# Low halves of 24 down-projection strips made by a negated copy on ACT and an adding SBUF-to-SBUF transfer

## The chip, the cores and the metric

The kernel runs on 1 core of one Trainium2 chip. The metric is the device time of one execution in microseconds (us). Three runs of the kernel before gave 1706.45, 1706.47 and 1707.92, so the median is 1706.47.

## What is computed

Two transformer blocks over 512 tokens of width 1024, all in float32. The first block has a gated MLP, a mixer (causal latent attention and a short convolution) and a second gated MLP; the second block has a mixer (Fourier, convolution, neighbourhood attention with a context) and a plain MLP. The change lies in that last MLP, whose core is

```python
hn = modulate_2(rms_norm_2(h_lat, norm2_g[i]), sh2, sc2)
h_lat = h_lat + g2 * (jnp.square(jax.nn.relu(hn @ mlp_w1[i])) @ mlp_w2[i])
```

with `mlp_w1` 1024 x 4096 and `mlp_w2` 4096 x 1024. A final RMS norm over the result is the output.

## The kernel before

Every large product is made in three passes on TensorE. A float32 value is split into a high half, rounded to the type float32r, and a low half, the value less its high half. TensorE then adds high weight x high activation, high weight x low activation and low weight x high activation (`products`, L779 to L781; for the seven products below L1316 to L1318).

**Strips.** Weights come in strips of 128 output columns: 128 partitions x 8 chunks x 128 columns, 512 KB. A strip has the running number u and the slot u % 4 in three rings of four: RAW (as loaded), W_HI and W_LO. Its way is: SP waits until the low half of strip u - 4 is ready and loads RAW (L571). ACT waits for the load and until TensorE is done with strip u - 4, and copies RAW to W_HI with rounding (`split_hi`, L1474; semaphore `hi_ready`). DVE subtracts, W_LO = RAW - W_HI (`split_lo`, L1958; for two strips in one instruction `split_pair`, L2492), and increments `lo_ready`. TensorE waits for `lo_ready` and for a free PSUM bank. The semaphores hi_ready and lo_ready count strips in order. ACT and DVE split three strips ahead (`LEAD`): `split_next(u0, it, j)` takes strip u0 + j + 3.

**The last MLP** is done in 4 parts of 1024 hidden columns. Each part has an up projection (8 strips of `mlp_w1`) and a down projection (8 strips of `mlp_w2`, starting at u + KC with u = U_MLP + 2 * KC * part). Part 0's up projection is made by plain strips: ACT makes the relu (L1798), DVE squares (L2559), ACT rounds (L1801), DVE subtracts (L2562). The up projections of parts 1 to 3 take strips in pairs, each pair by seven products of half size in place of eight (`seven_products`): DVE forms sums of weight quarters (`sum_weights`, L2481 to L2486, which also changes RAW in place at L2483), ACT rounds them, DVE subtracts (L2498). Three partial results are copied from PSUM to SG by ACT (`keep`, L1759); TensorE waits for these copies (`part_kept`) before it starts the third, fourth and fifth product, and DVE adds them back (L2504). Then ACT makes relu, square and rounding of the pair before (`finish_pair`, L1766 to L1788), and DVE the low halves (L2512, L2518).

The order on each engine is that of the program. In the last pair (i = 3) of parts 1 to 3 ACT does: keep 0, high half of down strip 0, keep 1, high half of down strip 1, keep 2, `finish_pair` of the pair before, `finish_pair` of the last pair, high half of down strip 2. During a down projection ACT splits strips 3 to 7 at j = 0 to 4, then the next up pair. DVE splits a strip, then updates X from the bank (L2545). In part 0's down projection DVE and ACT also prepare sums and differences of the normed activations for the seven products ("tau": DVE L2525 to L2531, ACT L1832, DVE L2538), for one chunk at each of j = 0 to 3; ACT's order there is high half of strip j + 3, then tau j. At j = 5 DVE makes the sums and the low halves of the next up pair, at j = 6 the low halves of the sums.

POOL (GpSimd) makes constants at the start and later only adds squares for the five norms (`sum_squares`, L756); the last of these runs in part 3's down projection. Nothing in the kernel before is loaded or stored by a DMA that POOL issues.

Of the kernel before, what the change touches and what calls it, by code (L numbers as in the profile page):

```python
# [5 lines left out]
F32 = mybir.dt.float32  # L6
F32R = mybir.dt.float32r
I32 = mybir.dt.int32
ALU = mybir.AluOpType
ACT = mybir.ActivationFunctionType  # L10
AX = mybir.AxisListType

P = 128
D = 1024
KC = D // P
# [5 lines left out]
H = 8  # L21
# [13 lines left out]
SPAN_IN = SPAN - SPAN % 16  # L35
# [8 lines left out]
RING = 4  # L44
# [19 lines left out]
U_MLP = U_OUT2 + KC  # L64
MLP_PARTS = 4
# [44 lines left out]
def block_pair_kernel(nc, a, out):  # L110

    with ExitStack() as ctx:
# [3 lines left out]
        def sb(name, shape, dt=F32, over=None):  # L116
            size = int(np.prod(shape[1:])) * 4
            offset = place[0] if over is None else over
            if over is None:
                place[0] += (size + 63) // 64 * 64  # L120
            t = nc.alloc_sbuf_tensor_at(name, shape, dt, offset=offset)
            where[name] = offset
            return t
# [12 lines left out]
        RAW = sb("RAW", [P, RING * STRIP])  # L136
        W_HI = sb("W_HI", [P, RING * STRIP], F32R)
        W_LO = sb("W_LO", [P, RING * STRIP], F32R)
# [71 lines left out]
        RPB = sb("RPB", [P, H * SPAN_IN + 16], over=scratch + 20 * 1024)  # L210
# [53 lines left out]
        def sem(name):  # L264
            return ctx.enter_context(nc.semaphore(name))

        raw_in = [sem(f"raw_in{i}") for i in range(RING)]
        hi_ready = sem("hi_ready")
        lo_ready = sem("lo_ready")
# [14 lines left out]
        const_ready = sem("const_ready")  # L284
# [58 lines left out]
        ctx_full = sem("ctx_full")  # L343
        chi_ready = sem("chi_ready")
        clo_ready = sem("clo_ready")
        flip_ready = sem("flip_ready")
        rpb_in = sem("rpb_in")
        table_in = sem("table_in")
        sig_ready = sem("sig_ready")
# [4 lines left out]
        ln_std = sem("ln_std")  # L354
        z_ready = sem("z_ready")
        act_ready = sem("act_ready")
        rpb_end = sem("rpb_end")
        table_split = sem("table_split")
        ut_mixed = sem("ut_mixed")
        swap_ready = sem("swap_ready")  # L360
# [44 lines left out]
        tau_hi = sem("tau_hi")  # L405
        tau_lo = sem("tau_lo")
        relu_done = sem("relu_done")
        EARLY, LATE = slice(0, HS), slice(HS, S)

        def chunk(t, k, n=S):  # L410
# [65 lines left out]
        def strip_of(t, slot):  # L476
            return t[:, slot * STRIP:(slot + 1) * STRIP]
# [246 lines left out]
        @block.gpsimd  # L724
        def _(pool):
            pool.memset(IDENT[:, :], 0.0).then_inc(pool_seq, 1)
            pool.memset(ONES[:, :], 1.0).then_inc(const_ready, 1)
            pool.memset(CONST[:, 0:1], EPS).then_inc(const_ready, 1)
            pool.memset(CONST[:, 1:2], LN_EPS).then_inc(const_ready, 1)
            pool.memset(CWIDE[:, :], 0.0).then_inc(const_ready, 1)  # L730
            pool.wait_ge(pool_seq, 1)
            pool.affine_select(out=IDENT[:, :], in_=IDENT[:, :], compare_op=ALU.not_equal, fill=1.0, base=0,
                               pattern=[[-1, P]], channel_multiplier=1).then_inc(ident_ready, 1)
            pool.wait_ge(ident_ready, 1)
            pool.tensor_tensor(SUM32[:, :], IDENT[:, 0:32], IDENT[:, 32:64], ALU.add).then_inc(pool_seq, 1)
            for i in (2, 3):
                pool.wait_ge(pool_seq, i)
                pool.tensor_tensor(SUM32[:, :], SUM32[:, :], IDENT[:, 32 * i:32 * i + 32], ALU.add).then_inc(pool_seq, 1)
            pool.wait_ge(pool_seq, 4)
            pool.sem_inc(const_ready, 1)  # L740
            pool.memset(FLIP[:, :], 0.0).then_inc(pool_seq, 1)
            pool.wait_ge(pool_seq, 5)
            pool.affine_select(out=FLIP[:, :], in_=FLIP[:, :], compare_op=ALU.not_equal, fill=-1.0, base=1 - P,
                               pattern=[[1, P]], channel_multiplier=1).then_inc(flip_ready, 1)
            sq, seq = Tally(sq_ready), Tally(pool_seq)
            seq.n = 5

            def sum_squares(clear):

                if clear:  # L750
                    pool.wait_ge(stat_ready, clear)
                pool.memset(SSUM[:, :], 0.0).then_inc(pool_seq, 1)
                pool.wait_ge(pool_seq, seq.add())
                for k in range(KC - 1):
                    pool.wait_ge(sq_ready, sq.add())
                    pool.tensor_tensor(SSUM[:, :], SSUM[:, :], SQ[:, k % 2 * S:(k % 2 + 1) * S], ALU.add).then_inc(pool_seq, 1)  # L756
                    pool.wait_ge(pool_seq, seq.add())
                    pool.sem_inc(sq_used, 1)
                sq.add()

            for norms in range(5):
                sum_squares(norms)
                if norms == 2:
                    pool.wait_ge(gem_done, T_2)
                    pool.memset(RPB[:, H * SPAN_IN:], 0.0).then_inc(rpb_end, 1)

        @block.tensor
        def _(pe):
# [220 lines left out]
            def ffn(u, after_up, after_down):  # L989
                for i, (_, chunks) in enumerate(FFN_PARTS):  # L990
                    if u == U_FFN0:
                        begin(u, H_HI, H_LO, normed())
                        strips(u + RING, 2 * chunks - RING, H_HI, H_LO)
                    elif i == 0:
                        new_strips(u, 2 * chunks, H_HI, H_LO, normed_halves(), first_halves)
                    else:
                        strips(u, 2 * chunks, H_HI, H_LO)
                    u += 2 * chunks
                    after_up[i]()
                    if u + KC == U_LATENT:  # L1000
                        strips(u, RING, A_HI, A_LO, chunks, each=widened(chunks))
                        for j in range(RING, KC - 1):
                            strip(u + j, (u + j) % RING, A_HI, A_LO, chunks)
                        last_halves(u + KC - 1, A_HI, A_LO, chunks)
                    else:
                        strips(u, KC, A_HI, A_LO, chunks, each=widened(chunks))
                    u += KC
                    after_down[i]()
# [147 lines left out]
            def mixer2():  # L1156
# [26 lines left out]
                def turn_biases(heads):  # L1183

                    for h in heads:
                        if h >= 5:
                            pe.wait_ge(bias_ready, h - 2)
                        pe.matmul(bank[BIAS_BANKS[h]][:, 0:SPAN], FLIP[:, :], RPB[:, h * SPAN_IN:h * SPAN_IN + SPAN],
                                  start=True, stop=True).then_inc(rpb_turned, 1)

                pe.wait_ge(table_in, 16 * (6 + ROWS))
                pe.wait_ge(bank_free, U_OUT2 + RING)
                pe.wait_ge(flip_ready, 1)
                pe.wait_ge(rpb_end, 1)
                turn_biases(range(2))
                turn_values(3)
                for t in range(2):
# [95 lines left out]
                for j in range(KC - 1):  # L1293
                    slot = (U_OUT2 + j) % RING
# [152 lines left out]
            for at, rows, n in ((16, ROWS1, V_ROWS), (128, ROWS2, M_CTX), (256, ROWS3, 2 * CK2)):  # L1447
# [13 lines left out]
            ffn(U_FFN1, [lambda: fold(64, M_2, T_ADA),  # L1461
                         nothing, lambda: fold(M_2, M_CTX, T_2)], [nothing, context, nothing])
            mixer2()
            mlp()
            tail()
# [3 lines left out]
        def _(act):  # L1469
            def split_hi(u, slot, turn):  # L1470

                act.wait_ge(raw_in[slot], turn * 16 + 16)
                act.wait_ge(strip_done, u + 1)
                act.activation(strip_of(W_HI, slot), strip_of(RAW, slot), ACT.Copy).then_inc(hi_ready, 1)  # L1474

            def split_next(u0, it, j):
                u = u0 + j + LEAD
                if not isinstance(it, int) or it * RING + u < STRIPS:
                    split_hi(it * RING + u, u % RING, it + u // RING)
# [414 lines left out]
            u = U_FFN0  # L1894
            for i, (_, chunks) in enumerate(FFN_PARTS):
                ffn_up(u, chunks)
                u += 2 * chunks
                down(u, 0 if i == 2 else None, True)
                u += KC
            mixer1()  # L1900
            norm_halves(48, U_OUT + KC)
            u = U_FFN1
            for i, (_, chunks) in enumerate(FFN_PARTS):
                ffn_up(u, chunks)
                u += 2 * chunks
                if i == 1:
                    act.wait_ge(ctx_in, 16)
                    for t in range(2):
# [4 lines left out]
                                   scale=1.0 / D).then_inc(ctx_std, 1)  # L1913
# [9 lines left out]
            def written(t):  # L1923
# [9 lines left out]
                           scale=1.0 / D).then_inc(tail_std, 1)  # L1933
# [7 lines left out]
                           scale=1.0 / D).then_inc(std_ready, 1)  # L1941
# [6 lines left out]
        def _(dve):  # L1948
# [5 lines left out]
                dve.wait_ge(dve_seq, seq.add())  # L1954

            def split_lo(u, slot):
                dve.wait_ge(hi_ready, u + 1)
                dve.tensor_tensor(strip_of(W_LO, slot), strip_of(RAW, slot), strip_of(W_HI, slot).bitcast(F32),  # L1958
                                  ALU.subtract).then_inc(lo_ready, 1)
# [528 lines left out]
            def split_pair(u):  # L2488

                at = slice(u % RING * STRIP, (u % RING + 2) * STRIP)  # L2490
                dve.wait_ge(hi_ready, u + 2)
                dve.tensor_tensor(W_LO[:, at], RAW[:, at], W_HI[:, at].bitcast(F32), ALU.subtract).then_inc(lo_ready, 2)  # L2492

            def split_sums(q):
# [296 lines left out]
```

## Time and profile before

| | |
|---|---|
| median of 3 runs | 1706.47 us |
| the profiled execution, its own time | 1709.55 us |
| its span | 1707.7 us |
| TensorE busy | 1682.7 us (99%) |
| DVE busy | 1148.6 us (67%) |
| ACT busy | 689.9 us (40%) |
| POOL busy | 67.3 us (4%) |

The profile comes from one execution. Busy time counts matmuls and other work, not waits or the issuing of DMAs. Durations of matmuls overlap, so their pace is read from their start times. In the rows, a line with an arrow says which line of which engine ended an engine's idle time. Part 0's down projection runs from 1400.0 to 1443.6 us, part 1's up projection to 1485.1 and its down projection to 1528.6; part 2's down projection starts at 1569.0, part 3's up projection at 1612.5.

### The profile page before, as it was taken

To read this page: it belongs to the slowest core of one execution; us is meant where nothing else is said; L and a number is where in the kernel's file an instruction comes from. 1 tells how busy PE (TensorE), PEld (TensorE's weight loads), DVE (VectorE), ACT (ScalarE), POOL (GpSimd) and SP (SyncE) were. 2 spreads that over 40 slices of the span, in tenths; PEclk is the share of its full clock that TensorE was granted. 3 is DMA by queue.
4 is the path that set the end of the run, shared out by engine and by line. 5 is a ranking of instruction groups with operands and counts; after the bars stand their busy time and mean duration, and the time that the engine had idled before them with its cause. 6 is when DMAs were issued, how large, how long until landed. Compare 5 with 4: busy or idle time off the path is not lost.

```text
span 1707.7 us, 24554 instructions
## 1 busy us (share of the span) xinstructions
PE 1682.7 (99%) x8956; PEld 1407.4 (82%) x8956; DVE 1148.6 (67%) x2096; ACT 689.9 (40%) x1048; POOL 67.3 (4%) x56
## 2 busy tenths in 40 slices
PE   7999999999999999999999999999999999999998
PEld 5788888888878868897888888888868988989897
DVE  3778578655655696469969973469675558756563
ACT  4421222234236573354222334342466443626262
POOL 0000000011000000200000000200000200000002
PEclk9999999999999999999999999999999999999999
DMA  9866566332523302537666632454200232434331
GB/s 331 254 207 197 178 202 211 109 102 57 141 74 98 99 1 75 172 106 219 190 204 188 175 113 80 116 167 112 87 1 17 83 112 74 116 87 124 85 108 50
DMA packets 355674, 218.59 MB, mean 128 GB/s; under 512 B 8544, under 2 KB 353668, under 8 KB 355588
## 3 DMA queue, kind: packets, MB, share of 16 engines
q1 hardware_dynamic: 355356, 217.37, 43.7%
q8 instruction: 52, 0.85, 0.2%
q14 instruction: 34, 0.28, 0.1%
q10 hardware_dynamic: 232, 0.09, 0.0%
HBM read 215.34 MB, written 2.11 MB: 127 GB/s over the span
## 4 chain that ended last, share of the span: by engine, by line
PE 91%; DVE 5%; ACT 1%; issue 1%; DMA 1%; SPq 0%; POOL 0%; DVEq 0%; ACTq 0%; POOLq 0%
PE bank L779 23%; PE bank L781 23%; PE bank L780 23%; PE bank L1316 2%; PE bank L1318 2%; PE bank L1317 2%; PE bank L1041 1%; PE bank L1025 1%; PE bank L957 1%; PE bank L961 1%; PE bank L958 1%; PE bank L1276 1%; DVE W_LO L1958 1%; DVE STAT L2172 1%; PE bank L1077 1%
## 5 line engine op out<-in xcount | busy, mean ns | idle before, releaser
L1474 ACT ACTIVATE W_HI<-RAW 128x1024 fp32r<-128x1024 f32 x278 | 292.3, 1055 | 458.7 <-PE bank L781 397.2
L779 PE MATMUL bank<-H_HI,W_HI 128*128 128x512 f32 x1090 | 425.6, 390 | 3.9 <-DVE W_LO L1958 3.8
L781 PE MATMUL bank<-H_HI,W_LO 128*128 128x512 f32 x1090 | 424.2, 389 | 0.0
L780 PE MATMUL bank<-H_LO,W_HI 128*128 128x512 f32 x1090 | 424.1, 389 | 0.0
L1958 DVE TENSOR_TENSOR W_LO<-RAW,W_HI 128x1024 fp32r<-128x1024 f32 x254 | 311.2, 1226 | 103.2 <-ACT W_HI L1474 100.0
L779 PE MATMUL bank<-A_HI,W_HI 128*128 128x512 f32 x714 | 279.4, 391 | 0.0
L780 PE MATMUL bank<-A_LO,W_HI 128*128 128x512 f32 x714 | 277.9, 389 | 0.0
L781 PE MATMUL bank<-A_HI,W_LO 128*128 128x512 f32 x714 | 277.9, 389 | 0.0
L779 PEld LDWEIGHTS bank<-H_HI,W_HI 128*128 128x128 f32 x1090 | 204.6, 188 | 49.3 <-issue 5.1
L781 PEld LDWEIGHTS bank<-H_HI,W_LO 128*128 128x128 f32 x1090 | 204.6, 188 | 42.6
L780 PEld LDWEIGHTS bank<-H_LO,W_HI 128*128 128x128 f32 x1090 | 204.6, 188 | 42.5 <-issue 0.2
L779 PEld LDWEIGHTS bank<-A_HI,W_HI 128*128 128x128 f32 x714 | 134.0, 188 | 28.4 <-issue 1.0
L781 PEld LDWEIGHTS bank<-A_HI,W_LO 128*128 128x128 f32 x714 | 134.0, 188 | 28.1
L780 PEld LDWEIGHTS bank<-A_LO,W_HI 128*128 128x128 f32 x714 | 134.1, 188 | 27.2
L1987 DVE SCALAR_TENSOR_TENSOR GACC<-GBUF,CSIL,GACC 128x256 f32<-128x256 f32 x360 | 147.5, 479 | 0.0
L756 POOL TENSOR_TENSOR SSUM<-SSUM,SQ 128x512 f32<-128x512 f32 x35 | 62.3, 1779 | 1590.7 <-ACT SQ L1485 1590.7
L2110 DVE TENSOR_TENSOR HF<-SG,bank 128x512 f32<-128x512 f32 x44 | 30.2, 686 | 127.9 <-PE bank L781 118.7
L1541 ACT ACTIVATE A_HI<-HF 128x512 f32 (+1 forms) x44 | 27.8, 633 | 204.2 <-DVE HF L2110 204.2
L2133 DVE SCALAR_TENSOR_TENSOR X<-bank,GHALF,X 128x512 f32<-128x512 f32 (+1 forms) x47 | 35.2, 748 | 39.2 <-PE bank L781 39.2
L2133 DVE SCALAR_TENSOR_TENSOR X<-bank,MOD,X 128x512 f32<-128x512 f32 x21 | 15.7, 749 | 58.3 <-PE bank L781 47.5
L2380 DVE SCALAR_TENSOR_TENSOR ACC<-CV,COL,ACC 128x512 f32<-128x512 f32 x60 | 45.0, 751 | 1.7
L2545 DVE SCALAR_TENSOR_TENSOR X<-bank,MOD,X 128x512 f32<-128x512 f32 x24 | 18.0, 748 | 40.9 <-PE bank L781 40.9
(432 smaller groups left out, 2311.6 us busy)
## 6 DMA issues: line engine op xcount, KB each, us to landing
RAW<-in_ffn_w SPq DMA_DIRECT2D x116, 512.0 KB, 4.9
GBUF<-in_w_ada SPq DMA_DIRECT2D x32, 1024.0 KB, 7.5
RAW<-in_mlp_w SPq DMA_DIRECT2D x64, 512.0 KB, 4.1
RAW<-in_w_in SPq DMA_DIRECT2D x57, 512.0 KB, 3.9
GBUF<-in_ada_w SPq DMA_DIRECT2D x24, 1024.0 KB, 7.2
RAW<-in_w_out SPq DMA_DIRECT2D x16, 512.0 KB, 3.9
RAW<-in_ffn_w SPq DMA_DIRECT2D x16, 384.0 KB, 3.4
PBUF<-in_w_ada SPq DMA_DIRECT2D x4, 1024.0 KB, 10.7
```

What stands on the lines that cost most here:

```text
L756: pool.tensor_tensor(SSUM[:, :], SSUM[:, :], SQ[:, k % 2 * S:(k % 2 + 1) * S], ALU.add).then_inc(pool_seq, 1)
L779: pe.matmul(dst, w_hi, x_hi, start=first and i == 0, stop=False)
L780: pe.matmul(dst, w_hi, x_lo, start=False, stop=False)
L781: mm = pe.matmul(dst, w_lo, x_hi, start=False, stop=last and i == len(blocks) - 1)
L1316: pe.matmul(dst, his[k], hi[k], start=first and k == 0, stop=False, skip_group_check=not first)
L1317: pe.matmul(dst, his[k], lo[k], start=False, stop=False, skip_group_check=not first)
L1318: mm = pe.matmul(dst, los[k], hi[k], start=False, stop=last and k == KC // 2 - 1, skip_group_check=not first)
L1474: act.activation(strip_of(W_HI, slot), strip_of(RAW, slot), ACT.Copy).then_inc(hi_ready, 1)
L1958: dve.tensor_tensor(strip_of(W_LO, slot), strip_of(RAW, slot), strip_of(W_HI, slot).bitcast(F32), ALU.subtract).then_inc(lo_ready, 1)
L1987: ins = dve.scalar_tensor_tensor(out=acc[k % 2], in0=g[:, k * GEM:(k + 1) * GEM], scalar=CSIL[:, vec + k:vec + k + 1], in1=acc[k % 2], op0 ...
L2133: dve.scalar_tensor_tensor(out=chunk(X, it * RING + j), in0=bank[(u0 + j) % RING][:, :], scalar=gate[:, bass.ds(it * RING + (gate0 + j), 1 ...
L2380: ins = dve.scalar_tensor_tensor(out=chunk(ACC, c), in0=v, scalar=tap, in1=chunk(ACC, c), op0=ALU.mult, op1=ALU.add)
```

## The change

For the 24 down strips of parts 0, 1 and 2 (the list `DOWNS`), DVE's subtraction is left out. After the high half, ACT waits for it to be complete and writes the negated high half into the strip's slot of W_LO. POOL waits for that, issues a DMA from SBUF to SBUF that adds RAW to W_LO in place, waits until it has landed, and increments `lo_ready`. Before the first strip of each part it also waits until all strips before it are counted. DVE waits for `lo_ready` before it splits the pair that follows a down projection, so that the count stays in order. Apart from this, two semaphores of constants (`flip_ready`, `rpb_end`) are merged into `const_ready`, which TensorE then awaits at 7. The transfers stand in POOL's program before the last sum of squares. The values computed are the same: -W_HI + RAW for RAW - W_HI.

```diff
--- before.py
+++ after.py
@@ -343,7 +343,6 @@
         ctx_full = sem("ctx_full")
         chi_ready = sem("chi_ready")
         clo_ready = sem("clo_ready")
-        flip_ready = sem("flip_ready")
         rpb_in = sem("rpb_in")
         table_in = sem("table_in")
         sig_ready = sem("sig_ready")
@@ -354,7 +353,6 @@
         ln_std = sem("ln_std")
         z_ready = sem("z_ready")
         act_ready = sem("act_ready")
-        rpb_end = sem("rpb_end")
         table_split = sem("table_split")
         ut_mixed = sem("ut_mixed")
         swap_ready = sem("swap_ready")
@@ -405,6 +403,9 @@
         tau_hi = sem("tau_hi")
         tau_lo = sem("tau_lo")
         relu_done = sem("relu_done")
+        neg_hi = sem("neg_hi")
+        lo_landed = sem("lo_landed")
+        DOWNS = [U_MLP + 2 * KC * part + KC + j for part in range(MLP_PARTS - 1) for j in range(KC)]
         EARLY, LATE = slice(0, HS), slice(HS, S)
 
         def chunk(t, k, n=S):
@@ -741,7 +742,7 @@
             pool.memset(FLIP[:, :], 0.0).then_inc(pool_seq, 1)
             pool.wait_ge(pool_seq, 5)
             pool.affine_select(out=FLIP[:, :], in_=FLIP[:, :], compare_op=ALU.not_equal, fill=-1.0, base=1 - P,
-                               pattern=[[1, P]], channel_multiplier=1).then_inc(flip_ready, 1)
+                               pattern=[[1, P]], channel_multiplier=1).then_inc(const_ready, 1)
             sq, seq = Tally(sq_ready), Tally(pool_seq)
             seq.n = 5
 
@@ -759,10 +760,19 @@
                 sq.add()
 
             for norms in range(5):
+                if norms == 4:
+                    for n, u in enumerate(DOWNS):
+                        slot = u % RING
+                        pool.wait_ge(neg_hi, n + 1)
+                        pool.dma_start(strip_of(W_LO, slot).bitcast(F32), strip_of(RAW, slot), accum_op=ALU.add).then_inc(lo_landed, 16)
+                        pool.wait_ge(lo_landed, 16 * (n + 1))
+                        if n % KC == 0:
+                            pool.wait_ge(lo_ready, u + RING)
+                        pool.sem_inc(lo_ready, 1)
                 sum_squares(norms)
                 if norms == 2:
                     pool.wait_ge(gem_done, T_2)
-                    pool.memset(RPB[:, H * SPAN_IN:], 0.0).then_inc(rpb_end, 1)
+                    pool.memset(RPB[:, H * SPAN_IN:], 0.0).then_inc(const_ready, 1)
 
         @block.tensor
         def _(pe):
@@ -1190,8 +1200,7 @@
 
                 pe.wait_ge(table_in, 16 * (6 + ROWS))
                 pe.wait_ge(bank_free, U_OUT2 + RING)
-                pe.wait_ge(flip_ready, 1)
-                pe.wait_ge(rpb_end, 1)
+                pe.wait_ge(const_ready, 7)
                 turn_biases(range(2))
                 turn_values(3)
                 for t in range(2):
@@ -1472,6 +1481,9 @@
                 act.wait_ge(raw_in[slot], turn * 16 + 16)
                 act.wait_ge(strip_done, u + 1)
                 act.activation(strip_of(W_HI, slot), strip_of(RAW, slot), ACT.Copy).then_inc(hi_ready, 1)
+                if isinstance(u, int) and u in DOWNS:
+                    act.wait_ge(hi_ready, u + 1)
+                    act.activation(strip_of(W_LO, slot), strip_of(W_HI, slot).bitcast(F32), ACT.Copy, scale=-1.0).then_inc(neg_hi, 1)
 
             def split_next(u0, it, j):
                 u = u0 + j + LEAD
@@ -1954,6 +1966,10 @@
                 dve.wait_ge(dve_seq, seq.add())
 
             def split_lo(u, slot):
+                if isinstance(u, int) and u in DOWNS:
+                    return
+                if isinstance(u, int) and u - 1 in DOWNS:
+                    dve.wait_ge(lo_ready, u + RING)
                 dve.wait_ge(hi_ready, u + 1)
                 dve.tensor_tensor(strip_of(W_LO, slot), strip_of(RAW, slot), strip_of(W_HI, slot).bitcast(F32),
                                   ALU.subtract).then_inc(lo_ready, 1)
@@ -2489,6 +2505,8 @@
 
                 at = slice(u % RING * STRIP, (u % RING + 2) * STRIP)
                 dve.wait_ge(hi_ready, u + 2)
+                if u - 1 in DOWNS:
+                    dve.wait_ge(lo_ready, u + RING)
                 dve.tensor_tensor(W_LO[:, at], RAW[:, at], W_HI[:, at].bitcast(F32), ALU.subtract).then_inc(lo_ready, 2)
 
             def split_sums(q):
```

## Rows read from the trace of the kernel before

**Rows 1.** The page: busy time of TensorE, and the two groups that split strips
```profile
PE 1682.7 (99%) x8956; PEld 1407.4 (82%) x8956; DVE 1148.6 (67%) x2096; ACT 689.9 (40%) x1048; POOL 67.3 (4%) x56
...
L1474 ACT ACTIVATE W_HI<-RAW 128x1024 fp32r<-128x1024 f32 x278 | 292.3, 1055 | 458.7 <-PE bank L781 397.2
...
L1958 DVE TENSOR_TENSOR W_LO<-RAW,W_HI 128x1024 fp32r<-128x1024 f32 x254 | 311.2, 1226 | 103.2 <-ACT W_HI L1474 100.0
```

**Rows 2.** Waits of TensorE, 1396 to 1660 us (us in total, times, longest)
```profile
PE bank L1316 <- ACT SG L1759: 0.6, 1, 0.6
```

**Rows 3.** Windows: us, busy PE, PEld, DVE, ACT, POOL (x count), clock, DMA share, GB/s
```profile
1400.00:1443.60 43.60, 43.60 (x194) 36.09 (x194) 32.58 (x45) 14.75 (x16) 0.00 (x0) 1.00 0.25 72
...
1485.10:1528.60 43.50, 43.50 (x194) 36.03 (x193) 20.48 (x22) 13.43 (x16) 0.00 (x0) 1.00 0.35 96
```

**Rows 4.** Timeline of TensorE (start us, us, engine line op, what, idle before)
```profile
1443.58 0.28 PE L1316 MATMUL bank<-H_HI,W_HI 128*128 128x256 f32 x1
...
1448.67 0.39 PE L1316 MATMUL bank<-H_HI,SUM_HI 128*128 128x256 f32 x1 [0.62 <-ACT SG L1759]
...
1479.33 0.28 PE L1316 MATMUL bank<-H_HI,SUM_HI 128*128 128x256 f32 x1
...
1480.77 0.28 PE L1316 MATMUL bank<-TAU_HI,SUM_HI 128*128 128x256 f32 x1
...
1485.09 0.40 PE L779 MATMUL bank<-A_HI,W_HI 128*128 128x512 f32 x1
```

**Rows 5.** Timeline of DVE, part 0's down projection and the pair after it
```profile
1411.15 1.23 DVE L1958 TENSOR_TENSOR W_LO<-RAW,W_HI 128x1024 fp32r<-128x1024 f32 x1 [1.86 <-ACT W_HI L1474]
1412.30 0.74 DVE L2545 SCALAR_TENSOR_TENSOR X<-bank,MOD,X 128x512 f32<-128x512 f32 x1
...
1416.34 0.42 DVE L2531 SCALAR_TENSOR_TENSOR TAU<-TAU,HSUM 128x256 f32<-128x256 f32 x1
1418.62 1.23 DVE L1958 TENSOR_TENSOR W_LO<-RAW,W_HI 128x1024 fp32r<-128x1024 f32 x1 [1.86 <-ACT W_HI L1474]
...
1445.19 0.75 DVE L2545 SCALAR_TENSOR_TENSOR X<-bank,MOD,X 128x512 f32<-128x512 f32 x1
...
1446.57 0.69 DVE L2483 TENSOR_TENSOR RAW<-RAW 128x512 f32<-128x512 f32 x1
```

**Rows 6.** Timeline of ACT: part 0's up projection, and first and last pair of part 1
```profile
1388.64 1.04 ACT L1474 ACTIVATE W_HI<-RAW 128x1024 fp32r<-128x1024 f32 x1
...
1448.26 0.36 ACT L1759 ACTIVATE SG<-bank 128x256 f32<-128x256 f32 x1
...
1476.65 0.38 ACT L1759 ACTIVATE SG<-bank 128x256 f32<-128x256 f32 x1 [3.19 <-PE bank L1318]
1476.93 1.05 ACT L1474 ACTIVATE W_HI<-RAW 128x1024 fp32r<-128x1024 f32 x1
1478.09 0.38 ACT L1759 ACTIVATE SG<-bank 128x256 f32<-128x256 f32 x1
...
1479.53 0.39 ACT L1759 ACTIVATE SG<-bank 128x256 f32<-128x256 f32 x1
...
1484.31 0.63 ACT L1776 ACTIVATE CROSS<-CROSS 128x512 f32<-128x512 f32 x1 [0.97 <-DVE CROSS L2504]
...
1487.65 1.99 ACT L1474 ACTIVATE W_HI<-RAW 128x1024 fp32r<-128x1024 f32 x2
```

**Rows 7.** The page: DMA issues, KB each and median us from issue to landing
```profile
RAW<-in_mlp_w SPq DMA_DIRECT2D x64, 512.0 KB, 4.1
...
GBUF<-in_ada_w SPq DMA_DIRECT2D x24, 1024.0 KB, 7.2
...
out<-YTOK SPq DMA_DIRECT2D x4, 512.0 KB, 3.0
CTOK<-in_ctx SPq DMA_DIRECT2D x1, 1024.0 KB, 6.2
```

**Rows 8.** POOL's additions (ns min/median/max)
```profile
L756 POOL TENSOR_TENSOR SSUM<-SSUM,SQ x35: 1287/1810/1987, 371.1 to 1694.4; 128x512 f32<-128x512 f32 x35
```

## The prediction, made before the changed kernel was run

> **What bounds the kernel now.** I read the page first. TensorE is busy for 1682.7 of 1707.7 us [rows 1], so only idle gaps of TensorE, 25 us in all, can be given back, and DVE (67%) and ACT (40%) count only where TensorE waits for them. The change touches the last MLP, so next comes the list of TensorE's waits there, from 1396 to 1660 us: one wait, 0.6 us, for the ACT copy of a partial product [rows 2]. The windows say the same: in the down projections of parts 0 and 1 TensorE is busy for all of the 43.6 and 43.5 us, with the granted clock at 1.00 (the level of 2.4 GHz) [rows 3]. There is almost nothing to win here, and the question is what the new path can cost.
>
> A strip of 24 matmuls takes 43.5 / 8 = 5.44 us; a pair of strips in an up projection takes seven products of 12 matmuls at 0.12 us, 10.08 us. In the TensorE timeline the fourth and fifth products of part 1's last pair begin at 1479.33 and 1480.77, 1.44 us apart, and the down projection at 1485.09 [rows 4].
>
> **DVE's side: what is removed.** 24 subtractions of 1.226 us [rows 1], 29.4 us of DVE. They matter only in part 0's down projection. There DVE's turn for one strip lasts 1418.62 - 1411.15 = 7.47 us, against TensorE's 5.44 [rows 5]: it waits for ACT's high half, subtracts, updates X, splits and makes a tau block, and ACT in turn rounds that tau block before the next high half. So DVE falls behind, and its last update starts at 1445.19 although the strip ended at 1443.6; the sum of raw weights that ACT waits for starts at 1446.57, ACT's next high half is late, its second kept product starts only at 1448.26 [rows 5, 6], and TensorE's fourth product starts at 1448.67 in place of 1443.58 + 4.32 = 1447.90 (0.77 us), with the first matmul at 0.22 in place of 0.12 us, and a smaller gap of the same sort at the fifth (0.35): 1.2 us in all. Without the subtraction DVE's turn is the rest of it, 1412.30 to 1416.34 + 0.42, 4.5 us [rows 5], and the wait for the tau high half (0.85 us on ACT, in part overlapped) still leaves it under 5.44. DVE then keeps up, the last update starts some 1.3 us earlier and the gap closes: -1.2 us. In parts 1 and 2 DVE is busy for 20 of 43.5 us [rows 3], and nothing is gained.
>
> **ACT's side: what is added.** 24 negated copies, of the shape of the high half, so 1.055 us each [rows 1], and each waits for the high half's completion first, some 0.1 us: 1.15 us a strip. In the down projection of part 0 ACT is busy for 14.75 of 43.6 us [rows 3], and that hides them. In part 0's up projection the first copy delays a relu by 1.1 us, which that relu's next wait for TensorE (1.66 us) absorbs. They are not hidden where strips 0 and 1 of the down projection are split between the kept products of the last pair, in parts 1 and 2 (part 3's down strips are not in the list). In order on ACT now [rows 6]: kept 0 at 1476.65, high half 1476.93 to 1477.98, kept 1 at 1478.09, high half, kept 2 at 1479.53. After the change: high half to 1477.98, negated copy 1478.08 to 1479.13, kept 1 at 1479.03 to 1479.41, so the fourth product starts at 1479.46, not 1479.33; with its slow first matmul 0.25 us. High half 1479.31 to 1480.36, negated copy 1480.46 to 1481.51, kept 2 ends at 1481.79, so the fifth product starts at 1481.84 where 1480.77 + 0.25 was due: 0.82, and 0.1 for its first matmul. Together 1.2 us a part, in two parts +2.4 us. The relu chain behind it starts at 1481.7 and not 1479.8, and its 3.5 us end at 1485.2, before the last pair's chain, which starts at 1484.31 [rows 6] plus the 1.2, so it costs nothing more. The bounds of this term: 0, if the kept copies have more room than the timeline shows, and 4.6, if each of the four copies costs its whole 1.15.
>
> **POOL and the DMA: what is added.** Each low half now needs a POOL-issued transfer that reads 512 KB of RAW and 512 KB of the negated half, and writes 512 KB. POOL handles them one at a time: wait for the copy, issue, wait for landing, increment. Call this L. No row shows such a transfer. From below: a 512 KB store out of SBUF lands 3.0 us after its issue. From above: a load of 1024 KB beside other traffic lands in 7.2 us. I take 5.2: the 3.0 plus what 512 KB more cost an undisturbed load, 6.2 for CTOK less about 4.0 for RAW (4.1 in the MLP) [rows 7]. How much time is there? Part 1, by the ACT times above, with the down projection starting at 1486.3 and strip j needed 5.44 j later:
> - Strip 0's copy is ready at 1479.1, so L may be 7.1.
> - Strip 2's high half is split with strip 3's from 1487.65 on [rows 6]; 1.2 us later, with the copy behind it, it is ready at 1491.0. Needed at 1497.1: L up to 6.1.
> - From there POOL's row of transfers counts. Strip 7, the sixth transfer from there, is needed at 1524.3: lateness 6L - 33.3, zero at L = 5.55. If strips 0 and 1 already push it, 8L - 45.2.
> - Part 0 begins earlier: strip 0's high half is split at 1388.64 [rows 6], the copy is ready at 1390.7, strip 7 is needed at 1438.1: 8L - 47.4, zero at 5.9.
>
> At 5.2 none of them is late, and the term is 0. Each RAW slot is refilled when its low half has landed, 4.1 us [rows 7]; the tightest refill (strip 6 in part 1) lands at 1491.0 + 5.2 + 4.1 = 1500.3, and ACT wants it at 1502.9. DVE has one new wait, before the pair behind each down projection, with the updates of strips 6 and 7 and the next sums queued behind it; in part 1 strip 7's copy is ready at about 1510.5 and lands long before 1521. SP's queue waits for the same landings. POOL has nothing else then; its next sum of squares is in part 3's down projection. The merged semaphores wait for events long past: 0.
>
> **The sum**: -1.2 + 2.4 + 0 = +1.2 us on this execution (1709.55 us, span 1707.7), 0.07%. The median of the runs is 1706.47, so 1707.6.
>
> **Rivals.**
> 1. POOL's row of transfers sets the pace (slower). It decides from L = 5.55 on in parts 1 and 2 and 5.9 in part 0. For it: my L is only 0.35 us under that, and every transfer runs beside loads that take 0.35 of the DMA engines [rows 3]. Against it: the transfer goes in long rows within SBUF, and the nearest 512 KB row takes 3.0. At L = 6.2: 2.2 + 2 x 4.4 = 11 us, 1718; at 7.2: 10.2 + 2 x 12.4 = 35, so 1743. The loss passes 0.2% from about L = 5.75. Chance 0.40.
> 2. POOL is held up by DVE. POOL's own additions of one shape take from 1287 to 1987 ns [rows 8], so something beside it costs up to 0.7 us. If that came onto the issue of each transfer, L = 5.9: 0 + 2 x 2.1 = 4.2, and 1.2, 1712. Chance 0.04. The Trainium skill (SBUF — State Buffer, "Who interferes with whom") speaks against the change here: POOL writes the descriptors of its DMAs, and shares a pair of SBUF ports with DVE under an exclusive lock. By the same section a DVE instruction with two SBUF inputs takes only the read side, and that page infers that descriptors need the write side; by that the subtractions around these transfers don't hold them.
> 3. DVE's relief is there and ACT's price is not: 1706.5 - 1.2 = 1705.3, same within the measurement. Chance 0.06, within "same". To get past 0.2% (3.4 us) faster, gaps would have to close that the waits don't list: 0.04.
>
> **How the numbers follow.** My forecast, no transfer late, has 0.46, with rival 3 beside it 0.52 for within 0.2%, about what a measurement of this kernel can tell from no change. Slower 0.44 (rivals 1 and 2), faster 0.04. The forecast's own range is 1705.3 to 1710. The whole range goes from 1705 to 1743, L = 7.2; beyond it I leave about 0.15 above and a few hundredths below.
>
> **What would show it.** POOL's queue: 24 transfers, each landing in about 5 us; over 5.5 is rival 1, and TensorE's waits then name the landing at the first matmul of down strips, from strip 2 on, growing to strip 7 in each part. The ACT steps: two waits of TensorE for SG, at the fourth and fifth product of the last pair, in parts 1 and 2, some 0.1 and 0.8 us; part 3 none. The DVE step: the wait at the first pair of part 1 is gone, and DVE's updates in part 0 come 5.4 us apart. I am wrong if L is over 5.8, if part 0's down projection has gaps of its own, or if loads of RAW become late behind the landings.

## The result, and the profile after

The changed kernel takes 1736.66 us (median of 4 runs, 1734.22 to 1737.08) against 1706.55 (median of 4), a ratio of 1.0172 with a 95% interval of 1.016 to 1.0185: 1.7% slower. The forecast was 1707.6 with a range of 1705 to 1743, so the time lies in the range, at its first rival and not at the forecast. Both profiled executions (spans 1707.7 and 1735.2 us) have a mean granted clock of 0.91 in their first 40 us, long before the changed code, while executions with 1.00 there are some 3 us shorter (spans of 1708.4 and 1705.6 us in runs 6 and 2 below), so the change is best read between the two profiled ones: 27.5 us, of the 30.1 us between the medians.

The page of the changed kernel, its busy time (to be read beside [rows 1]), its queues and its DMA issues:

```profile
span 1735.2 us, 24601 instructions
...
PE 1688.2 (97%) x8956; PEld 1405.7 (81%) x8956; DVE 1120.4 (65%) x2072; ACT 714.7 (41%) x1072; POOL 88.1 (5%) x80
...
q1 hardware_dynamic: 355356, 217.37, 43.2%
q0 software_dynamic: 3456, 12.58, 3.7%
...
RAW<-in_mlp_w SPq DMA_DIRECT2D x64, 512.0 KB, 4.3
...
W_LO<-RAW POOLq DMA_DIRECT2D x24, 512.0 KB, 6.5
```

DVE gave up 28 us of work and ACT took 25, as planned, and the kernel is slower all the same. The new row is the last: 24 transfers, each landing 6.5 us (median) after its issue.

The waits of TensorE from 1396 to 1690 us, where [rows 2] had one of 0.6 us:

```profile
PE bank L789 <- POOLq L771: 20.5, 17, 1.7
PE bank L1325 <- ACT SG L1771: 1.2, 2, 0.6
PE bank L789 <- DVE X L2563: 0.8, 1, 0.8
```

L771 is POOL's increment of `lo_ready` after a landing. The third row is one of the same stalls (strip 2 of part 1), put down to what came last by the profile. The stalls cost more than the rows say. The list has 18 gaps of 21.3 us in all, but the down projections of parts 0 to 2 grew by 7.9, 9.1 and 9.6 us, 26.6 in all. The rest, 0.3 us a gap, is the overlap of two matmuls that is lost and a slower first matmul behind the gap.

POOL's queue in part 0 and at the start of part 1 (start us, us of the issue, and the idle time before it with its releaser):

```profile
1390.97 1.01 POOL L767 DMA_DIRECT2D W_LO<-RAW  x1 [41.54 <-ACT W_LO L1486]
1396.23 0.86 POOL L767 DMA_DIRECT2D W_LO<-RAW  x1 [4.25 <-POOLq L771]
1404.28 0.86 POOL L767 DMA_DIRECT2D W_LO<-RAW  x1 [7.19 <-ACT W_LO L1486]
1411.33 0.86 POOL L767 DMA_DIRECT2D W_LO<-RAW  x1 [6.19 <-DMA W_LO<-RAW]
1418.38 0.86 POOL L767 DMA_DIRECT2D W_LO<-RAW  x1 [6.19 <-DMA W_LO<-RAW]
1425.22 0.86 POOL L767 DMA_DIRECT2D W_LO<-RAW  x1 [5.98 <-DMA W_LO<-RAW]
1432.12 0.86 POOL L767 DMA_DIRECT2D W_LO<-RAW  x1 [6.04 <-DMA W_LO<-RAW]
1439.16 0.86 POOL L767 DMA_DIRECT2D W_LO<-RAW  x1 [6.18 <-DMA W_LO<-RAW]
1486.03 0.86 POOL L767 DMA_DIRECT2D W_LO<-RAW  x1 [46.01 <-ACT W_LO L1486]
1491.12 0.86 POOL L767 DMA_DIRECT2D W_LO<-RAW  x1 [4.22 <-POOLq L771]
```

The first transfer of a part frees POOL after 5.26 and 5.09 us, the later ones come about 7.0 us apart. TensorE's timeline follows them, one gap for each strip of part 0 from strip 3 on (from strip 2 on in part 1, from strip 1 on in part 2):

```profile
1417.99 0.49 PE L789 MATMUL bank<-A_HI,W_HI 128*128 128x512 f32 x1 [1.32 <-POOLq L771]
1424.94 0.47 PE L789 MATMUL bank<-A_HI,W_HI 128*128 128x512 f32 x1 [1.22 <-POOLq L771]
1431.73 0.49 PE L789 MATMUL bank<-A_HI,W_HI 128*128 128x512 f32 x1 [1.07 <-POOLq L771]
1438.77 0.49 PE L789 MATMUL bank<-A_HI,W_HI 128*128 128x512 f32 x1 [1.31 <-POOLq L771]
1445.86 0.49 PE L789 MATMUL bank<-A_HI,W_HI 128*128 128x512 f32 x1 [1.38 <-POOLq L771]
```

Last, ACT between the kept products of part 1's last pair, which answers to [rows 6], and the starts of the fourth and fifth product:

```profile
1483.32 0.38 ACT L1771 ACTIVATE SG<-bank 128x256 f32<-128x256 f32 x1 [3.18 <-PE bank L1327]
1483.60 1.05 ACT L1483 ACTIVATE W_HI<-RAW 128x1024 fp32r<-128x1024 f32 x1
1484.68 1.06 ACT L1486 ACTIVATE W_LO<-W_HI 128x1024 fp32r<-128x1024 f32 x1
1485.65 0.37 ACT L1771 ACTIVATE SG<-bank 128x256 f32<-128x256 f32 x1
1485.91 1.05 ACT L1483 ACTIVATE W_HI<-RAW 128x1024 fp32r<-128x1024 f32 x1
1486.99 1.06 ACT L1486 ACTIVATE W_LO<-W_HI 128x1024 fp32r<-128x1024 f32 x1
1487.96 0.37 ACT L1771 ACTIVATE SG<-bank 128x256 f32<-128x256 f32 x1
```

```profile
1485.88 0.28 PE L1327 MATMUL bank<-TAU_HI,SUM_LO 128*128 128x256 f32 x1
1486.07 0.38 PE L1325 MATMUL bank<-H_HI,SUM_HI 128*128 128x256 f32 x1
1486.29 0.28 PE L1326 MATMUL bank<-H_LO,SUM_HI 128*128 128x256 f32 x1
...
1488.38 0.39 PE L1325 MATMUL bank<-TAU_HI,SUM_HI 128*128 128x256 f32 x1 [0.62 <-ACT SG L1771]
```

Kept 1 ends at 1486.02, and the fourth product starts 0.05 us later, at 1486.07, where 1486.00 was due; its first matmul takes 0.22 us to the next in place of 0.12. Together that is 0.17 us, too little for the list of waits. Kept 2 ends at 1488.33, and the fifth product starts 0.05 us later, 0.79 us after its time. By the starts of the strips the whole difference of the two profiled executions is accounted for, stage by stage:

| stage | before, us | after, us | difference |
|---|---|---|---|
| down projection, part 0 (its end) | 1443.58 | 1451.45 | +7.9 |
| up, part 1 | 41.51 | 41.34 | -0.2 |
| down, part 1 | 43.55 | 52.62 | +9.1 |
| up, part 2 | 40.31 | 41.35 | +1.0 |
| down, part 2 | 43.55 | 53.17 | +9.6 |
| up, part 3 | 40.31 | 40.31 | 0 |

The sum is 27.4 of 27.5 us. Part 2's up projection shows ACT's price alone, 1.0; in part 1 the same 1.0 and DVE's relief make -0.2, so the relief is 1.2. (Runs 4 and 8 below show the relief alone: part 1's up projection takes 40.31 us in place of 41.51.)

### The profile page after: what moved, and what is told of

It reads as the page before. It is cut to its first block and busy times, and to the rows that moved or that the text cites. A ratio compares the mean times of both kernels' runs of the same rounds, so it can differ in the third digit from the quotient of the medians.

```text
span 1735.2 us, 24601 instructions
## 1 busy us (share of the span) xinstructions
PE 1688.2 (97%) x8956; PEld 1405.7 (81%) x8956; DVE 1120.4 (65%) x2072; ACT 714.7 (41%) x1072; POOL 88.1 (5%) x80
## 3 DMA queue, kind: packets, MB, share of 16 engines
q1 hardware_dynamic: 355356, 217.37, 43.2%
## 5 line engine op out<-in xcount | busy, mean ns | idle before, releaser
L1974 DVE TENSOR_TENSOR W_LO<-RAW,W_HI 128x1024 fp32r<-128x1024 f32 x230 | 282.1, 1227 | 85.4 <-ACT W_HI L1483 82.1
L789 PE MATMUL bank<-A_HI,W_HI 128*128 128x512 f32 x714 | 281.4, 394 | 21.3 <-POOLq L771 20.5
```

The costliest lines, as they stand in the source:

```text
L789: pe.matmul(dst, w_hi, x_hi, start=first and i == 0, stop=False)
```

## The experiments

The question is where the 7.0 us come from, when the first transfer of a part took 5.1. Edits are against the changed kernel. The first four ran beside each other with the kernel before at 1706.52 us (33 runs), the last four with it at 1706.54 (21 runs).

**1. No transfer.** ACT's copy stays, POOL only counts.

```diff
-                        pool.dma_start(strip_of(W_LO, slot).bitcast(F32), strip_of(RAW, slot), accum_op=ALU.add).then_inc(lo_landed, 16)
-                        pool.wait_ge(lo_landed, 16 * (n + 1))
```

> The transfers are left out: POOL counts a strip as soon as the negated copy is there, so the low half of 24 strips is the negated high half alone. What is left of the change is DVE's relief (-1.2 us by the first pair of part 1) and ACT's copies between the kept products (+1.04 us in each of parts 1 and 2 by the changed kernel's trace). Theory (the whole loss is the transfers' pace): 1706.55 - 1.2 + 2.1 = 1707.4 us, no wait of TensorE in the down projections. Rival (the negated copies hold up ACT in the down projections too, and part of the 30 us is theirs): over 1712 us, with waits of TensorE for ACT or DVE in the down projections.

Measured: 1707.45 us (11 runs), ratio 1.0002, interval 0.9993 to 1.0011. TensorE's waits in the stretch are a single row:

```profile
PE bank L1323 <- ACT SG L1769: 1.2, 2, 0.6
```

The whole loss is the transfers'. Without them the two small terms come out as the stages above give them, to 0.1 us in the median (the interval is wider than that).

**2. Short loads.** The transfers are whole, the loads that their landings release are an eighth (64 KB).

```diff
-                load_strips(u, KC, lambda m: w_mlp1[:, :, bass.ds(m * P + part * D, P)])
-                load_strips(u + KC, KC, lambda m: w_mlp2[:, part * KC:(part + 1) * KC, bass.ds(m * P, P)])
+                if part == 0:
+                    load_strips(u, KC, lambda m: w_mlp1[:, :, bass.ds(m * P + part * D, P)])
+                else:
+                    for m in range(KC):
+                        n = 1 if m < RING else KC
+                        load_strip(u + m, (u + m) % RING, w_mlp1[:, 0:n, m * P + part * D:m * P + part * D + P])
+                for m in range(KC):
+                    n = 1 if m >= RING and part < MLP_PARTS - 1 else KC
+                    load_strip(u + KC + m, (u + KC + m) % RING, w_mlp2[:, part * KC:part * KC + n, m * P:m * P + P])
```

> The RAW loads that a landing releases (down strips 4 to 7 of parts 0 to 2, up strips 0 to 3 of parts 1 to 3) bring 64 KB in place of 512 KB; the rest of those tiles keeps what was there. The transfers themselves are as in the changed kernel. Theory A (a transfer takes 5.1 us alone, and 7.0 because the load that the transfer before it released runs beside it): POOL's transfers come 5.1 to 5.4 us apart, TensorE doesn't wait for them, 1707 to 1709 us. Theory B (7.0 us is the transfer's own time in the down projections, by adding, by POOL or by DVE's use of the port, and the shorter first one is the exception): 7.0 us apart, 1736 us.

Measured: 1707.45 us (10 runs), ratio 1.001, interval 1.0001 to 1.002. The last four transfers of part 2 in POOL's queue, and the landing times of all 24:

```profile
1581.88 0.86 POOL L774 DMA_DIRECT2D W_LO<-RAW  x1 [4.21 <-DMA W_LO<-RAW]
1586.93 0.86 POOL L774 DMA_DIRECT2D W_LO<-RAW  x1 [4.19 <-DMA W_LO<-RAW]
1592.00 0.86 POOL L774 DMA_DIRECT2D W_LO<-RAW  x1 [4.21 <-DMA W_LO<-RAW]
1597.05 0.86 POOL L774 DMA_DIRECT2D W_LO<-RAW  x1 [4.18 <-DMA W_LO<-RAW]
...
DMA to landing us min/median/max: 4.5/4.5/5.5
```

5.06 us apart and not 7.0, and no wait of TensorE for a landing: theory A. The transfer is the same, beside the same DVE and ACT work; what is gone is seven eighths of the load beside it. That load is there each time because the landing itself lets SP refill the slot, at the moment at which POOL issues the next transfer.

The DMA packets in the two traces show where the 2.0 us go. In the changed kernel SP issues the load some 0.35 us before POOL issues the next transfer (at 1417.84 strip 3 of part 0 is counted, at 1418.03 the load is issued, at 1418.38 the transfer), and the load's packets start some 0.7 us after POOL's issue. The transfer's own start 2.6 us after it (median of the 21 that have a load beside them) and the last one ends at 6.2. With the short loads they start at 1.4 us and end at 4.2 (medians of 24). So the load goes first and costs the transfer 1.1 us before its first packet, and 0.8 to 0.9 us more from there on. The three transfers that open a part have no load packets beside them in the changed kernel either, and land after 4.5 to 4.6 us.

DVE's work is there in both runs, so it is not what makes 7.0 of 5.06, and rival 2 of the prediction falls as a cause of the loss. Four of the 24 landings of this run take 4.7 to 5.5 us with no larger load beside them; why stays open.

**3. Two in flight.** POOL issues the next transfer, then waits for the one before. Further lines, not shown, give the transfers two semaphores in turn; the second one is freed by letting the load of CTOK count on `up_in`.

```diff
...
+                    def landed(n):
+                        pool.wait_ge((lo_landed, lo_second)[n % 2], 16 * (n // 2 + 1))
+                        pool.sem_inc(lo_ready, 1)
...
+                        else:
+                            landed(n - 1)
+                        if n % KC == KC - 1:
+                            landed(n)
```

> POOL issues a transfer before it waits for the landing of the one before, on two semaphores in turn, and computes the same values. By the queue's row the 24 transfers keep the 16 DMA engines busy for 3.7% of 1735.2 us, 2.7 us each, and a load for 1.7 us, together 4.4 of the 5.44 us of a strip. Theory (most of the 7.0 us is latency that POOL waits out one transfer at a time): no wait of TensorE for a landing, 1707 to 1709 us. Rival (the DMA engines are the limit when loads run beside): landings still come 6 us and more apart, 1715 to 1737 us.

Measured: 1711.0 us (10 runs), ratio 1.0021, interval 1.0012 to 1.0031: between the two, 26 us better than the change and 3.5 worse than without transfers. TensorE waits for a landing twice, at strip 2 of parts 1 and 2:

```profile
PE bank L795 <- POOLq L766: 3.0, 2, 1.5
PE bank L1331 <- ACT SG L1777: 1.2, 2, 0.6
```

Strips 2 and 3 come to ACT together behind the relu chain, their transfers were issued at 1487.02 and 1489.07, and strip 2 was counted only at about 1494.5. Two things meet there. One is POOL's order in this run: strip 1, whose packets had ended at 1482.65, is counted only once strip 2's copy is ready, at 1487.01, so that the load behind it is issued at 1487.21, beside strip 2's transfer. The other is that more now runs at once: the first packet of strip 2's transfer comes 3.3 us after its issue, and the load of an MLP strip lands in 5.1 us (median), not 4.1. ACT waits for loads, which it does neither in the kernel before nor in the changed one; this is its row for part 1 (1480 to 1530 us), and part 2 has the same three waits:

```profile
ACT W_HI L1489 <- DMA RAW<-in_mlp_w: 11.5, 3, 6.1
```

So most of the loss was latency that POOL waited out one transfer at a time. The 3.5 us that stay belong to strip 2 of parts 1 and 2; how much of them is POOL's order and how much the sharing, this run does not part.

**4. Strips 3, 5 and 7 only.**

```diff
-        DOWNS = [U_MLP + 2 * KC * part + KC + j for part in range(MLP_PARTS - 1) for j in range(KC)]
+        DOWNS = [U_MLP + 2 * KC * part + KC + j for part in range(MLP_PARTS - 1) for j in (3, 5, 7)]
...
```

By further lines, not shown, POOL also waits, before it counts each of these strips, until all strips before it are counted.

> Only down strips 3, 5 and 7 of parts 0 to 2 are made by the transfer, the others by DVE's subtraction; the values are the same. A transfer then has 10.9 us, and no negated copy lies between the kept products. Theory (pace alone): no wait of TensorE for a landing, the first pair's gap of part 1 is gone, 1706.55 - 1.2 = 1705.3 us. Rival (DVE, which has to wait for each landing before it counts the next strip, is late in its turn): gaps in the down projections, the relief is lost, 1707 us or more.

Measured: 1705.54 us (11 runs), ratio 0.9996, interval 0.9987 to 1.0005. TensorE has no wait between 1390 and 1690 us. The median is 1.0 us below the kernel before, near the 1.2 expected, but the interval takes in 1. Part 1's up projection is 1.2 us shorter, and part 0's down projection 0.25 us longer (43.77 us for 43.52): strip 7 starts 0.1 us late, behind a transfer issued at 1430.45, with a slow first matmul, which is too little for the list.

**5. A plain copy**, the same transfer without `accum_op`.

> The transfer copies RAW over the negated half and adds nothing, so the low half of 24 strips is the raw tile. The loads are whole. Theory (adding has its price: it reads 512 KB more, and its 2.7 us of the 16 engines are half as long for a copy): transfers 5 to 5.5 us apart beside loads and not 7.0, the waits of TensorE for landings all but gone, 1707 to 1712 us. Rival (adding costs nothing beside POOL's issue and the latency, and the load beside it makes the rest): 7.0 us apart, 1734 us or more.

Measured: 1709.51 us (8 runs), ratio 1.0016, interval 1.0006 to 1.0026; TensorE waits for landings twice, 0.8 us in all. The landing times:

```profile
DMA to landing us min/median/max: 2.8/5.5/5.8
```

The issues come 6.1 us apart beside loads, more than the 5 to 5.5 expected and less than 7.0. Without the adding the period is 0.9 us shorter, though still longer than TensorE's 5.44.

**6 and 7. Nearly alone: the plain copy, and adding half the size**, both with the short loads of run 2. "Alone" below means beside a load of 64 KB at the most.

> The plain copy of the run before, with the short loads of 64 KB, so that nothing runs beside it: landing of a copy alone, where adding took 4.5 us. Theory (adding costs the second read): 3 to 3.7 us. Rival (fixed latency and POOL make nearly all of it): 4.2 to 4.5 us. The total is 1707.4 us by either.

> Adding transfers of 256 KB (the first half of each strip; the other half stays the negated copy) with the short loads. The fixed part of the 4.5 us to landing is then seen: if the fixed part is 2 us and the data 2.5, landing takes 3.2 to 3.3 us; if it is mostly fixed, 4 us and more; if all of it is data, 2.3 us. The total is 1707.4 us by each.

Measured in one execution each: 1710.15 us (with 0.91 in its first 40 us) and 1707.14. The landing rows, of the plain copy first, then of the 256 KB:

```profile
DMA to landing us min/median/max: 2.8/2.9/3.9
```

```profile
DMA to landing us min/median/max: 3.2/3.3/3.9
```

Alone, an adding transfer lands after 4.5 us for 512 KB and 3.3 for 256 KB; a line through these two points has 2.1 fixed and 1.2 for each 256 KB. A plain copy takes 2.9, so adding costs 1.6 us by itself. A load beside it adds 2.0 to the adding transfer (6.5 less 4.5) and 2.6 to the plain one (5.5 less 2.9). The Trainium skill (DMA: Bandwidth & Descriptors, "Anatomy of one DMA — SWDGE (gpsimd) path") gives 2.0 us and the bytes over 436 GB/s; for the adding transfer the runs agree with it if both tiles that are read count as bytes: 1.05 MB in 2.4 us is 437 GB/s (400 to 480, as the landings are read to 0.1 us). For the plain copy 3.2 us is the estimate from the same figures of the page, and 2.9 was measured.

**8. Strips 3, 5 and 7 of part 0 only.** As run 4 with `range(1)` for the parts.

> Only strips 3, 5 and 7 of part 0's down projection, three transfers in the whole kernel; the same values. Theory (DVE's relief is worth something in part 0 alone, and it is the gap at the first pair of part 1): as with strips 3, 5 and 7 of all parts, 1705.5 us, no wait of TensorE in the last MLP. Rival (parts 1 and 2 gave part of it): 1706 us or more.

Measured: 1705.62 us (11 runs), ratio 0.9999, interval 0.999 to 1.0008; no wait of TensorE in the stretch. Three transfers do what nine do, by medians and by spans (1703.5 and 1703.7 us, against 1705.5 for run 1, whose ACT copies lie between the kept products). No version beats the kernel before by more than the measurement can tell. By the stages there is 1.2 us to have here; these two have it, and give 0.2 of it back at strip 7 of part 0 (43.73 us in this run).

## Why the prediction came out as it did

- **DVE's relief, -1.2 us**: right in size and place. The first pair's gap is gone, run 8 gets the gain from part 0 alone, and DVE's first updates in part 0 come 5.4 and 5.7 us apart in place of 6.6 and 7.5, until the landings pace them.
- **ACT's price, +1.2 us a part**: 1.0 measured. Both gaps are there: 0.17 us at the fourth product, where the sum had 0.25, and 0.79 and 0.1 at the fifth, where it had 0.82 and 0.1.
- **The transfer, L = 5.2**: here the forecast failed. Alone, L is 5.06 from issue to issue, so the term was near for what it priced, a transfer with nothing beside it. Some of that is luck: the 5.2 was added up from landing times, and alone the landing takes 4.5; the 0.5 us from a landing to the next issue, which no term held, made up for most of the difference. But I priced it with "what 512 KB more cost an undisturbed load", looked at the load that a landing releases only for whether the load would be late, and put the traffic beside it at an average share of 0.35. The load starts when the next transfer does, every time, and makes L 7.0. The step that failed is that term, by 1.8 us, and with it the step built on it, that no transfer is late.
- **What L does to the time**: the row of transfers (rival 1) held. For 7.0 the formulas give 8.6, 10.8 and 10.8 us late; the starts of the strips show 7.9, 9.1 and 9.6. They are a little less because the first transfer of a part has no load beside it and takes 5.1 to 5.3. It is the lateness that grows toward strip 7, as forecast; the gaps themselves are of like size, 0.6 to 1.7 us, one for each strip.
- **The edges**: the loads of RAW did not become late in the changed kernel; the merged semaphores cost nothing that the stages show. DVE did wait for the last landing of each part before the pair behind it (15.0 us in three waits), and that cost nothing, since TensorE waited for the same landing.

The forecast gave 0.40 to the case that came, and 0.46 to its own. With 0.35 us between L and the point at which it decides, and an end of the range at 7.2 beside loads, the case with loads beside every transfer deserved to be the forecast.

## What to carry to other kernels

Where a transfer's landing frees a buffer, the refill starts at once and runs beside the next transfer: price the transfer with that load beside it, at every turn, not with the mean share of the queue. In a chain that handles transfers one at a time, compare the period under load with the period of the consumer; 7.0 against 5.44 us costs at every step, while three or nine transfers with room between them cost 0.2 us. Work taken from an engine off the critical path (28 us of DVE) was worth only the one gap that it caused, 1.2 us.

## What was not expected of the hardware

- A DMA of 512 KB that adds in SBUF lands 4.5 us after its issue alone, a plain copy of the same size after 2.9; POOL's issue takes 0.86 us for the adding one and 0.53 for the copy.
- A load of 512 KB beside it costs the transfer 2.0 to 2.6 us, more than the 1.8 us for which a load keeps the 16 engines busy (43.2% of 1735.2 us for the 217.37 MB of its queue, a load being 0.52 MB). Of the 2.0 us of the adding one 1.1 pass before its first packet: the load has its packets under way 0.7 us after POOL's issue, the transfer only after 2.6 us.
